# Mixtures of experts: one-hot selection of rows for four experts by matmuls of 256 columns, and two weight units of the last expert kept in the turned-activation buffer

## What is computed

```python
g_idx = argmax(x @ w_grp + b_grp)                  # one of 4 groups
top_v, top_i = top_k(expert_logits[g_idx], 2)      # two of its 8 experts
for each expert e, for its rows xb:
    y = (silu(xb @ w_gate[e]) * (xb @ w_up[e])) @ w_down[e]
out[token] += weight[token, e] * y
```

## Time and profile before

| | |
|---|---|
| median of 3 runs | 2167.49 us (2164.78 to 2170.81) |
| the profiled execution | 2171.3 us, of which the span of its instructions is 2169.2 us |
| busy | PE 2003.0 us (92%), PEld 1076.1, DVE 675.6, ACT 404.9, POOL 118.6 |
| transfers | 593.39 MB, mean 274 GB/s |
| stages by their first and last matmul | mixture 0: 377.4 to 857.6 us; mixture 1: 1039.6 to 1520.5; mixture 2: 1886.7 to 2140.3 |
| mean granted TensorE clock | 0.969 of 2.4 GHz |

### The profile page before, as it was taken

One profiled execution on the slowest core, in us unless ns is written; L12 is line 12 of the kernel. 1 busy time (PEld: TensorE's weight loads), 2 busy tenths in 40 slices (PEclk: granted clock), 3 DMA queues, 4 the chain that ended last, 5 costly groups with the idle time before them and its releaser, 6 DMA issues.

```text
span 2169.2 us, 25934 instructions
## 1 busy us (share of the span) xinstructions
PE 2003.0 (92%) x10197; PEld 1076.1 (50%) x10197; DVE 675.6 (31%) x1571; ACT 404.9 (19%) x873; POOL 118.6 (5%) x141
## 2 busy tenths in 40 slices
PE   8999989999999998799999999999599989999873
PEld 4444446545545454645544545545444445665442
DVE  0154547211111111635311111111637223532123
ACT  1133432111111111111111111111233222112112
POOL 0000000100000000000100000000100001021100
PEclk9999999999999999899999999999798989999997
DMA  9511102999999999712799999999721111599995
GB/s 317 165 39 39 39 23 98 355 419 421 421 420 420 421 421 363 268 63 94 271 419 420 421 421 421 421 420 402 269 84 39 39 39 30 188 344 414 420 420 238
DMA packets 121892, 593.39 MB, mean 274 GB/s; under 512 B 15857, under 2 KB 41345, under 8 KB 58847
## 3 DMA queue, kind: packets, MB, share of 16 engines
q1 hardware_dynamic: 108495, 565.96, 65.8%
q0 software_dynamic: 13328, 26.49, 3.7%
HBM read 572.95 MB, written 35.44 MB: 280 GB/s over the span
## 4 chain that ended last, share of the span: by engine, by line
PE 82%; DMA 11%; DVE 4%; ACT 2%; issue 1%; SPq 0%; ACTq 0%; DVEq 0%; POOLq 0%
PE bank L854 19%; PE bank L839 12%; PE bank L597 10%; PE bank L881 10%; DMA ring<-in_w_up_dram 5%; PE bank L739 4%; PE bank L609 4%; DMA ring<-in_moe_w_up_dram 4%; PE bank L927 3%; PE bank L583 3%; PE bank L967 1%; PE bank L1096 1%; PE bank L693 1%; PE bank L830 1%; PE bank L666 1%
## 5 line engine op out<-in xcount | busy, mean ns | idle before, releaser
L854 PE MATMUL bank<-ring,work 128*64 128x512 f32 x2048 | 451.4, 592 | 1.8 <-DMA ring<-in_moe_w_up_dram 1.4
L854 PEld LDWEIGHTS bank<-ring,work 128*64 128x64 f32 x2048 | 146.7, 137 | 293.2 <-issue 292.5
L839 PEld LDWEIGHTS bank<-work 128*128 128x128 f32 x2240 | 260.1, 191 | 57.0 <-issue 52.3
L839 PE MATMUL bank<-work 128*128 128x128 f32 x2240 | 285.6, 281 | 0.0
L1706 DVE TENSOR_TENSOR work<-work,bank 64x512 f32<-64x512 f32 x64 | 67.8, 1060 | 612.5 <-ACT work L1227 612.5
L597 PE MATMUL bank<-hT,ring 128*128 128x512 f32 x512 | 238.5, 609 | 0.7 <-ACT work L1159 0.7
L881 PE MATMUL bank<-ring,work 128*64 128x512 f32 x1024 | 233.8, 598 | 0.0
L597 PEld LDWEIGHTS bank<-hT,ring 128*128 128x128 f32 x512 | 94.3, 194 | 110.0 <-issue 108.2
L927 PE MATMUL bank<-ring,work 128*64 128x256 f32 x1024 | 116.9, 380 | 25.2 <-DMA ring<-in_w_up_dram 24.8
L1232 ACT ACTIVATE work<-bank 64x512 f32<-64x512 f32 x64 | 37.8, 590 | 484.7 <-PE bank L881 475.6
L881 PEld LDWEIGHTS bank<-ring,work 128*64 128x64 f32 x1024 | 67.6, 136 | 117.5 <-issue 109.8
(11 more groups left out here) (293 smaller groups left out, 1875.6 us busy)
## 6 DMA issues: line engine op xcount, KB each, us to landing
ring<-in_moe_w_gate_dram SPq DMA_DIRECT2D x128, 1024.0 KB, 17.4
ring<-in_moe_w_up_dram SPq DMA_DIRECT2D x128, 1024.0 KB, 19.6
ring<-in_moe_w_down_dram SPq DMA_DIRECT2D x128, 1024.0 KB, 17.8
ring<-in_w_gate_dram SPq DMA_DIRECT2D x32, 1024.0 KB, 21.1
ring<-in_w_up_dram SPq DMA_DIRECT2D x32, 1024.0 KB, 22.4
ring<-in_w_down_dram SPq DMA_DIRECT2D x32, 1024.0 KB, 21.7
ring<-in_attn_w_qkv_dram SPq DMA_DIRECT2D x12, 1024.0 KB, 13.4
work<-y_rows SPq DMA_DIRECT2D x12, 1024.0 KB, 8.7
```

Of the source, the lines that this page charges most:

```text
L839: mm = pe.matmul(XT[half][:, P * k:P * k + width], src[:, tt, c0:c0 + P], sel[buf][:, tt, 0:width], start=(tt == 0), stop=(tt == T - 1))
L854: mm = pe.matmul(GU[BLK * a:BLK * a + BLK, :], xT_[:, 4 * kk + k, :], v[:, k, :], start=(kk + k == 0), stop=(kk + k == 4))
```

## The change

It has two parts. (1) **Rows are selected for four experts at a time.** A matmul now has 256 columns (`QUAD`), and each of the four experts of a quad turns one quarter of the next quad: 2 chunks of 128 features, 8 matmuls (`turn_group`). In mixtures 0 and 1 the whole group stands ahead of the wait for `hg`; only in expert 0 it stands behind the transposes, since there `turn_second_pair` (32 matmuls of 128 columns for experts 2 and 3) comes first. Experts 28 to 31 turn nothing. In mixture 2 all rows are selected like this: the gathers, their transposes, `x_rows` and the DMAs that wrote it are gone. The loops have bodies of eight experts and run three times. (2) **Two units of expert 31 do not pass through the ring**: `load_spare` brings them into `hT` once the router has read it, right behind the loads of the first experts. Each mixture has two ring units fewer.

```diff
-    units += [None] * (E * 6)
+    units += [None] * (E * 6 - SPARE)
...
+                def turn_second_pair():
+                    pe.wait_ge(main.sel, main.sel0 + 1)
+                    for half in range(2):
+                        turn_rows(main, half, P, P)
+
+                def turn_group(i, s, par):
+                    if s == 0:
+                        pe.wait_ge(main.sel, main.sel0 + 2 + i)
+                    pe.wait_ge(main.xT, main.x0 + 3 + s + TURN * i)
+                    for k in range(2):
+                        for tt in range(T):
+                            c0 = P * (2 * s + k)
+                            mm = pe.matmul(XT[s % 2][:, QUAD * k:QUAD * k + QUAD], src[:, tt, c0:c0 + P],
+                                           sel[1 - par][:, tt, :], start=(tt == 0), stop=(tt == T - 1))
+                    mm.then_inc(main.xt, 1)
...
                     if ahead is not None:
-                        ahead(range(3))
+                        ahead(0)
                     pe.wait_ge(b.hg, b.n0 + j + 1)
...
                     if ahead is not None:
-                        ahead(range(3, 4))
+                        ahead(1)
                     pe.wait_ge(b.hT, b.n0 + j + 1)
...
+                    def ahead(part):
+                        if first_one and part == 0:
+                            turn_second_pair()
+                        elif part == first_one and not (type(i) is int and i == E // TURN - 1):
+                            turn_group(i, s, par)
...
+                def ahead2(i, s, par):
+                    if type(i) is int and TURN * i + s == 0:
+                        turn_group(i, 0, par)
+                    if type(i) is not int or TURN * i + s < E - TURN - 1:
+                        turn_group(i + 1 if s == TURN - 1 else i, (s + 1) % TURN, (par + (s + 1) // TURN) % 2)
...
+                    if type(i) is int and TURN * i + s == 1:
+                        load_spare()
+
+                def load_spare():
+                    sp.wait_ge(routing.logits, T * (l + 1))
+                    sources = expert_units(m, l, E - 1)
+                    for a in range(SPARE):
+                        src = next(sources)
+                        dst = spare[a] if l < 2 else spare[a].rearrange("p a n -> p (a n)").rearrange("p (k n) -> p k n", k=K)
+                        sp.dma_start(dst, src).then_inc(spare_loaded, 16)
...
-                    expert(main, j, lambda: copy_rows(main, (pair + 1) % 2, s % 2, j + 3, P))
-                    if s % 2:
-                        select(pair % 2, j + 3)
+                    def ahead():
+                        if type(i) is int and j == 0:
+                            copy_second_pair()
+                        copy_group(i, s, par)
+
+                    expert(main, j, None if type(i) is int and i == E // TURN - 1 else ahead)
+                    if s == 2 and not (type(i) is int and i == E // TURN - 1):
+                        select(par, j + 6, 0, TURN)
...
-                if l == 2:
-                    for tt in range(T):
-                        pool.wait_ge(tiles_written, turns["rms1"].src0 + tt + 1)
-                        pool.dma_start(x_rows[2 * P * tt:2 * P * tt + 2 * P, :].rearrange("(p k) d -> p k d", k=2),
-                                       hn[:, tt, :].unsqueeze(1).to_broadcast([P, 2, D])).then_inc(x_stored, 16)
...
-                    if l == 2 and 6 <= q + 4 < E // 2:
-                        gather_rows(q + 4)
```

More of the change, by code:

```diff
@@ L15 @@
 TURN = 4
+QUAD = TURN * BLK
+SPARE = 2
 UNITS = 12
@@ L369, in program @@
         rms0_gain = wk(3072, D)
-        xg = [wk(9216 + 2048 * i, D) for i in range(2)]
         def dealt(v, k):
@@ L484, in load2, with slot @@
                     sp.dma_start(ring[u % UNITS][:, :], src).then_inc(unit_loaded[u % UNITS], 16)
-                def slot(i, s):
+                def slot(i, s, par):
                     gate, up, down = (a.rearrange("e (p k) n -> e p k n", p=P) for a in expert_weights)
-                    if not last_slot(i, s):
+                    if gu_in_ring(i, s):
                         load2(i, 3 * s + 2, gate[TURN * i + s + 1])
                         load2(i, 3 * s + 3, up[TURN * i + s + 1])
-                    load2(i, 3 * s + (2 if last_slot(i, s) else 4), down[TURN * i + s])
+                    load2(i, down_unit(i, s), down[TURN * i + s])
+                    if type(i) is int and TURN * i + s == 2:
+                        load_spare()
                 if l < 2:
-                    over_blocks(sp, body)
+                    over_quads(sp, body)
                 else:
@@ L831, in turn_block, with turn_rows @@
                     return pe.transpose(out, rows, eye)
-                def turn_rows(b, buf, half, width, ks=range(4)):
-                    for k in ks:
+                def turn_rows(b, half, lo, width):
+                    for k in range(4):
                         for tt in range(T):
@@ L839, in turn_rows, with expert @@
                             mm = pe.matmul(XT[half][:, P * k:P * k + width], src[:, tt, c0:c0 + P],
-                                           sel[buf][:, tt, 0:width], start=(tt == 0), stop=(tt == T - 1))
-                    if ks[-1] == 3:
-                        mm.then_inc(b.xt, 1)
-                def expert(b, j, xT_, turned_, unit, need, ahead):
+                                           sel[0][:, tt, lo:lo + width], start=(tt == 0), stop=(tt == T - 1))
+                    mm.then_inc(b.xt, 1)
+                def turn_second_pair():
[12 more added lines that the diff above has]
+                    mm.then_inc(main.xt, 1)
+                def expert(b, j, xT_, turned_, unit, need, ahead, in_spare=False):
                     pe.wait_ge(b.xT, b.x0 + turned_)
@@ L917, in unit2, with gate_up2 @@
                     return ring[u % UNITS][:, :]
-                def gate_up2(i, s):
-                    pair, of_pair = s // 2, s % 2
-                    pe.wait_ge(main.xT, main.x0 + TURN * i + 2 * pair + 2)
-                    v0 = 0 if type(i) is int and i + s == 0 else 3 * s - 1
-                    v = [unit2(i, v0 + a).rearrange("p (k n) -> p k n", k=K) for a in range(2)]
+                def gate_up2(i, s, par):
+                    b, quad = BLK * (s % TURN), (par + s // TURN) % 2
+                    in_ring = gu_in_ring(i, s - 1)
+                    pe.wait_ge(main.xT, main.x0 + (2 if type(i) is int and TURN * i + s < 2 else 4) +
+                               TURN * (s // TURN) + TURN * i)
+                    v0 = 0 if type(i) is int and TURN * i + s == 0 else 3 * s - 1
+                    if in_ring:
+                        v = [unit2(i, v0 + a).rearrange("p (k n) -> p k n", k=K) for a in range(2)]
+                    else:
+                        pe.wait_ge(spare_loaded, 16 * SPARE * (l + 1))
+                        v = [spare[a].rearrange("p k n -> p (k n)").rearrange("p (k n) -> p k n", k=K) for a in range(2)]
                     for k in range(K):
@@ L1257, in mixture @@
                 if l < 2:
-                    over_blocks(act, body)
+                    over_quads(act, body)
                 else:
                     product2(0, 0)
-                    over_slots(act, slot)
+                    over_quads(act, slot)
                 act.wait_ge(routing.indices, 2 * m.l + 2)
@@ L1749, in mixture @@
                 if l < 2:
-                    over_blocks(dve, body)
+                    over_quads(dve, body)
                 else:
-                    over_slots(dve, slot)
+                    over_quads(dve, slot)
                 dve.wait_ge(routing.indices, 2 * m.l + 2)
```

212 lines of the change are left out of this document (106 added, 106 removed).

## The result

The changed kernel takes **2238.9 us** (median; 2232.1 to 2246.0) against 2167.3 us of the kernel before (2164.8 to 2170.8): ratio 1.033, 95% interval 1.0294 to 1.0365. The prediction said 2208.0 us, range 2196 to 2219: the right sign, and 31 us too little. A second set of runs of the same kernel gave 2236.3 us, ratio 1.032 (1.0299 to 1.0341). The profiled execution is the fastest of its set: 2232.05 us, span 2229.8 us.

A forecast was written before the change was run, and what follows sets the result against it. TensorE was taken to bound mixtures 0 and 1 narrowly and mixture 2's start, transfers the rest. Terms 36.5 + 5.2 - 1.2 = +40.5 us on the 2167.5 us median gave 2208.0 us, range 2196 to 2219.

The forecast's parts named there:

- The unit price: TensorE's selection: a 256-column record at half the 512-column price, 0.2147 us; a group of 16 records 3.43 us.
- Slots 27 to 30 at 6.12 us: Mixture 2: these four slots turn no group and take 6.12 us each, 24.5 us in all.
- Expert 0: Mixtures 0 and 1: second pair, handoffs and group take 12.24 us where 3.96 stood, +8.3 us a mixture.
- VectorE's stall: Expert 0, mixtures 0 and 1: TensorE may wait for VectorE's unexplained 2.4 us stall; 0 to 2.4, taken as 1.2 each.
- The bare handoff: Mixtures 0 and 1: TensorE idles 0.53 us ahead of down while VectorE copies hT, cancelling the group's 0.53 us saving.
- experts 28 to 31: Mixtures 0 and 1: no turning saves 3.96 us each, idle steps add 1.89 and 0.53; four times, -6.2 us a mixture.
- mixture 2 at TensorE's pace: Mixture 2: without the gather, transfers stay hidden and TensorE's slots of 9.17 us set the length, 290.2 us, +36.5.
- The transfer waits: Mixtures 0 and 1: TensorE's 1.4 us of waits vanish, as it reaches expert 28 later and part 2 advances transfers.
- Part 2 brings nothing of its own: Mixtures 0 and 1: the spare units' transfers end 2 us earlier net, but transfers don't bind, so no gain.
- The transfers' pace: Mixtures 0 and 1: weight transfers take 2.547 us a unit, 15.28 us an expert, 0.32 us slower than TensorE.
- instruction fetch: Rival, eight-expert loops: entering a body costs TensorE 2.4 us, twelve times, 29 us in all; 2237 us, chance 0.08.
- price per instruction: Rival, all mixtures: a 256-column record costs 0.118 us like one of 128, and transfers set the pace; 2148 us, chance 0.04.

The follow-up runs named there:

- e3: Changed kernel with a quarter of each group put behind the transposes in mixtures 0 and 1: 2220.5 us, ratio 1.0246.
- r1: The changed kernel itself, run again without any edit: 2236.3 us, ratio 1.032.
- e2: Kernel before with mixture 2's gather replaced by its own selection matmuls of 128 columns in every slot: 2209.5 us, ratio 1.0199.
- e11: Kernel before with only one of four token tiles in each selection, so three quarters of the tokens are missing from the experts' input: 2152.3 us, ratio 0.9926.
- e6: Kernel before with only the two spare units added (last expert's gate and up units in hT): 2164.3 us, ratio 0.9989.
- e8: Kernel before with selection matmuls in two column halves and the two spare units: 2155.1 us, ratio 0.9949.
- e10: Changed kernel with the gather back in mixture 2, a quarter of each group behind the transposes, and groups in column halves: 2175.6 us, ratio 1.0045.
- e5: Kernel before with each 128-column selection matmul made as two of 64 weight columns: 2161.5 us, ratio 0.9978.
- e4: Changed kernel with each matmul of the four-expert selection made as two of 64 weight columns: 2219.9 us, ratio 1.0249.
- e7: Changed kernel with the gather back in mixture 2 and a quarter of each group behind the transposes: 2175.7 us, ratio 1.0051.
- e1: Changed kernel with mixture 2 as before the change, rows gathered; mixtures 0 and 1 and spare units stay changed: 2189.4 us, ratio 1.0109.
- e9: Changed kernel with quads 5 and 6 written out, so slot 27 of mixture 2 turns no unused group: 2229.5 us, ratio 1.0294.

## Why the prediction was right in direction and wrong in size

The three stages grew by 65.6 us in the profiled executions where 41.7 were predicted (5.2 + 36.5). By the prediction's own steps:

- **The unit price, the step that failed.** "A group of 16 records is 3.43 us" took a pure price by columns (0.2147 us; 0.216 by e3) for a stretch that also pays at both ends, where the matmuls go from 64 weight columns to 128 and back. The group is 3.65 us. The saving was worked out against a half of 3.96 us, read from the timeline *with* its four steps of 0.1 us: one side of the subtraction held the steps, the other did not. 0.216 x 16 + 0.2 against 0.111 x 32 + 0.4 leaves 0.3 us (3.65 and 3.96 in the rows), not 0.53. With the 0.52 handoff, and 0.06 us more at the transposes, an expert costs +0.28 us instead of 0.0: 27 experts, two mixtures, **15 us**. In mixture 2, 27 slots at 0.23 us more: **6 us**. The row that would have warned was in the earlier trace rows: 24 records in 2.87 us and 8 in 1.09 give (2.87 - 1.09) / 16 = 0.111 us a record and 0.2 us a piece. I divided stretches by their counts.
- **Slot 27.** "Slots 27 to 30 at 6.12 us" was a misreading: inside the loop the slot number is not known when the program is built, so its last round also turns a group. **3 us**, measured by taking it out (2.9).
- **The clock in the tail.** Not considered. One down in each of mixtures 0 and 1 took 1.3 to 1.4 us more at a lowered clock: **2.7 us** (3.3 in r1, two downs in mixture 1). Before the change TensorE had no idle step of this kind there.
- **Expert 0** was right: 8.3 us. The 1.2 us set aside in each mixture for VectorE's stall were too much, **-2.4 us**: the changed kernel's trace has no such stall. VectorE's copies of `hT` (394.19 us) and of the second pair (394.53) follow each other, TensorE waits 1.20 us for both, and no wait of VectorE ends in "remote". Nor does one in e2, whose mixtures 0 and 1 are the kernel before's; of the fourteen traces only that of the kernel before and e11's have it. What makes it stays open.
- **The bare handoff** (0.53 predicted, 0.52), **experts 28 to 31** (13.42 predicted; 841.01 - 827.60 = 13.41 in the timeline), and **mixture 2 at TensorE's pace** (share 0.83) were right. **The transfer waits** vanished as predicted, but e2 has none either, with neither of the two reasons given. The 1.2 us for an earlier load of `y_rows` did not come.
- **Part 2 brings nothing of its own:** right, for the reason given; e6 and e8 show both sides of it. The transfers' pace was read too slow: 15.28 us an expert from two waits, while the 420 GB/s from 400 to 800 us of the kernel before are 15.0 us for six units of 1.05 MB. TensorE and the transfers ran level. The margin of "about 4 us" to the transfers was 4.6 by e11. The emptied queue behind expert 0 was put at 3 us more; it is 7, which did no harm in the changed kernel since TensorE was slower still, and decided e10.

These sum to 15.1 + 6.2 + 2.9 + 2.7 - 2.4 = 24.5 us, of 23.9 between 41.7 and 65.6. The fit is in part luck: in mixtures 0 and 1 the terms give 15.4 us of 14.0, in mixture 2 9.1 of 9.8. From the stages to the spans it is -5.0 us (mainly the stretch between mixtures 1 and 2), 60.6 us; and from the spans to the medians +11, since the profiled execution of the kernel before lay 4.0 us above its median and that of the changed kernel 6.9 below its own: 71.6 us. I take these last steps for scatter between executions, not for terms of the change; by r1 the loss is 2236.3 - 2165.8 = 70.5 us. The rival nearest to the measured time, instruction fetch at 2237 us, was right by accident: the loops turn without a gap on TensorE, as the 9.40 us mean of 27 slots against 9.39 of one shows, and the 2.4 us that its price rested on is the stall of VectorE that is gone. The Trainium skill (TensorE: Matmul & The Clock Gate, Back-to-back issue gap) gives spacings of 81 and 131 ns for 128 and 512 columns, whose flat rise was the reason for the rival "price per instruction"; the records here, 0.111, 0.216 and 0.429 us, rise with the columns, and the measurement decides.

## What to carry to other kernels

Price a matmul from two stretches of different length, so that the slope gives the record and the intercept the cost of entering and leaving; never divide one stretch by its count and subtract it from another kind of stretch. Where TensorE and the transfers run within 1% of each other, cheaper TensorE work is worth only the margin, and an edit that helps one of them alone shows little. Against the 479.4 us of e6's two windows, the spare units alone took off nothing in mixtures 0 and 1, column halves alone 2.0 us in both together (e5), and the pair 7.3 (e8). A start that delays the first release of buffers costs the transfers' idle time in full once they are the bound.

## What the runs showed of the hardware

- **Going from 64 weight columns to 128 and back costs 0.1 us each way.** That is what TensorE loses between f32 matmuls on 64 weight columns (two side by side) and matmuls on all 128: 85 groups lost 16 to 19 us by it in the medians (e4), and four steps an expert were 0.46 of 14.96 us (e5). A 128 x 128 product made as two column halves side by side costs little more than the whole record, 0.222 us a pair against 0.216 for 256 columns and 0.113 against 0.111 for 128 (e4, e5), and avoids the steps.
- **In the tail the clock falls in single downs, in varying number.** Where experts 28 to 31 turn nothing, with idle steps of 1.76 and 0.52 us in 13.4 us, single downs took 5.0 to 5.4 us, two in e7 6.6, instead of 3.65. Mixtures 0 and 1 had one each in the changed kernel's trace, in e1 and in e9, none and two in r1, two and two in e4, two and three in e3, three and two in e7 and e10. The kernels that turn rows in the tail had none. But in e11 TensorE was idle for 15% of the stretch from 400 to 840 us, in steps of 0.4 to 1.3 us, and the granted clock stayed at 1.00. What makes the difference stays open.
- **The transfers hold 419 to 420 GB/s for hundreds of us** (400 to 840 us in e11, at a share of 1.01), with TensorE busy for 85% of the time, and the same 420 GB/s with TensorE busy for all of it (400 to 800 us of the kernel before).
